# Residual folded into the gathered rows of each expert, and the pair rows summed by one constant matrix

## The chip, the cores and the metric

One Trainium2 core of one chip. The metric is the device time of the kernel in microseconds, the median of several runs.

## The reference

One decoder layer on x of 512 tokens by 1024, float32. A hybrid mixer (an input projection of 1024 by 2560, a gated linear recurrence and a short gated convolution, an output projection) is added to alpha times x and normalised, which gives h. Then the expert layer: each token picks one of four groups, two of its eight experts, and gets their weighted sum.

```
weights = softmax(top2 logits of the group) * p(group)
hid = silu(t @ w_gate[e]) * (t @ w_up[e]) * combine[:, e]
ffn = sum over the 2 chosen e of hid @ w_down[e]        # 32 experts, 1024 -> 256 -> 1024
out = layer_norm(alpha * h + ffn, ln2_g, ln2_b)         # alpha = 2 ** 0.25
```

## The kernel before, in words

The first 175 us are the mixer, in float32 split into two parts, and the router. Then TensorE builds tables of rows by products of one-hot matrices: for each expert, up to 64 tokens (`BLOCK`), each as two half rows of 512 numbers, so 128 partitions. What does not fit goes to overflow items in a loop whose count is known only at run time; it is 0 in the profiled execution.

Each of the 32 experts is an *item*, with the same instructions on every engine. `x_rows` says which rows of `h1_rows` in DRAM an item reads, `y_rows` which rows of `y_pairs` it writes. The items 0 to 9 and the last ones are written out, the others run in a hardware loop (`rounds`). On TensorE (`pe_item`, L1141) item q is: `turn_x` of item q + 1 (four transposes of the gathered rows, L1092), `gate_up` of q (L1102), `down` of q - 1 (L1131) and `turn_hid` of q (L1122). ScalarE does the silu (L841) and copies the result y to `ys` (L848). VectorE copies the transposes and multiplies hid (L1469, L1541, L1546). GpSimd gathers the rows of later items (L676, `gather`) and scatters y (L681, `scatter`), with two buffers for each; gather i + 2 waits only until x of item i has been turned. Item 0 differs: its rows come from SBUF by a product, not by a gather. In item 2 TensorE also sums the overflow tables (L1059), and VectorE takes them (`take_over`, L1523), which is the third and fourth count of `rows_ready`. VectorE computes the routing weights in item 3 (`take_weights`).

The weights of an expert are three loads of 1 MB each, issued by SP's queue: gate and up into one of eight slots (`wgu`), down into one of nine buffers (`wdn`; `wdn_once` is used by one expert only, the ninth). `refill_gu(q)` (L555) waits until gate_up of item q - 8 is done, `refill_dn(q)` (L559) until a down is done: the refills of down up to item 16 ask for one down less than the others. SP issues in the order gu8, gu9, dn9, gu10, dn10, gu11 and so on; the last ones are gu31, dn30, dn31. Behind these SP loads h1 back (2 MB), waits for a scatter of item 28 and loads the two tables of the second layer norm, then waits for all scatters and loads the 8 blocks of y_pairs (0.5 MB each). A DMA waits in the queue behind those issued before it.

The end: alpha h1 is summed into eight PSUM banks by a diagonal matrix (L1193), each pair row times its weight by eight more diagonal matrices (L1200), one of them by VectorE (L1580). Then VectorE, ScalarE and GpSimd do the layer norm tile by tile (four tiles of 128 tokens) and SP stores.

## Time and profile before

| what | value |
|---|---|
| runs | 430.11, 430.84, 432.84 us; median 430.84 |
| profiled execution | span 432.4 us; its own time is not given apart from the span |
| TensorE busy | 410.6 us (95%), mean granted clock 0.979 |
| VectorE, ScalarE, GpSimd busy | 186.8 us (43%), 114.5 (26%), 83.1 (19%) |
| DMA | 139.11 MB, 322 GB/s on average; indirect and other GpSimd DMAs 11.84 MB |
| ScalarE's copies of y (L848) | 32, 597 ns each |
| GpSimd's longest wait at the start, for the first weights | 11.1 us |
| chain that ended last | PE 82%, DMA 11%, DVE 5% |

Times are in microseconds from the start of the span. PE is the products of TensorE, PEld its weight loads, DVE VectorE, ACT ScalarE, POOL GpSimd, SP the sync engine, a q behind a name the engine's queue of DMA issues. The clock is a share of full speed (1.00 is 2.4 GHz). The DMA share of a stretch is the mean busy share of the 16 DMA engines.

### The profile page before, as it was taken

The numbers are of one execution on the slowest core, as the hardware profiler recorded it, in microseconds if no ns is written. First come the engines' busy times: TensorE is split into PE (matmuls) and PEld (weight loads), VectorE is DVE, ScalarE is ACT, GpSimd is POOL, SyncE is SP. The second block draws the span as 40 slices with busy tenths as digits, with TensorE's granted clock in tenths as the row PEclk, the third lists the DMA queues.
The fourth block names the chain that finished last, engine by engine and source line by source line (L and its number), as shares of the span: only waits on it lengthen the run. The fifth ranks groups of instructions, "written<-read, shape, count | busy, mean of one in ns | idle before, by whom it ended". The sixth has DMA issues, their size and how long they took to land.

```text
span 432.4 us, 6542 instructions
## 1 busy us (share of the span) xinstructions
PE 410.6 (95%) x2578; PEld 277.1 (64%) x2578; DVE 186.8 (43%) x368; ACT 114.5 (26%) x185; POOL 83.1 (19%) x111
## 2 busy tenths in 40 slices
PE   6999999999999999989999999999999999788883
PEld 5888877888888888955555555556555655454331
DVE  1578722499957467855322122212222221111077
ACT  3524376973122002310111111111111111003211
POOL 2201000000000001011332333233223322110124
PEclk8999999999999999998999999999999999898997
DMA  8766340230369999999999999999999999999584
GB/s 266 220 222 208 126 146 28 93 97 31 114 218 420 425 418 420 422 407 378 403 418 413 418 411 412 417 414 411 418 416 417 418 418 416 418 417 416 196 352 194
DMA packets 37377, 139.11 MB, mean 322 GB/s; under 512 B 5107, under 2 KB 17427, under 8 KB 25062
## 3 DMA queue, kind: packets, MB, share of 16 engines
q1 hardware_dynamic: 31184, 126.89, 73.7%
q0 software_dynamic: 6144, 11.84, 7.5%
q8 instruction: 18, 0.29, 0.3%
q10 hardware_dynamic: 22, 0.02, 0.0%
q14 instruction: 9, 0.07, 0.0%
HBM read 134.41 MB, written 12.58 MB: 340 GB/s over the span
## 4 chain that ended last, share of the span: by engine, by line
PE 82%; DMA 11%; DVE 5%; issue 1%; ACT 0%; SPq 0%; DVEq 0%; POOLq 0%
PE bank L1102 24%; PE bank L915 12%; PE bank L917 12%; PE bank L916 12%; PE bank L1131 11%; DMA wgu_first<-in_exp_w_up 7%; PE bank L1092 3%; PE bank L1122 3%; DMA xg<-h_rows,x_rows 2%; DVE stats L1585 1%; DMA pair_y<-y_pairs 1%; PE bank L1012 1%; DMA raw<-in_w_in 1%; PE bank L1024 1%; PE bank L975 1%; PE bank L898 1%
## 5 line engine op out<-in xcount | busy, mean ns | idle before, releaser
L1102 PE MATMUL bank<-wgu,xTg 128*64 128x256 f32 x736 | 87.7, 392 | 3.3 <-DMA wgu<-in_exp_w_up 2.4
L1102 PEld LDWEIGHTS bank<-wgu,xTg 128*64 128x64 f32 x736 | 52.6, 141 | 31.0 <-issue 3.6
L915 PE MATMUL bank<-xT_hi,w_hi 128*128 128x512 f32 x160 | 63.2, 395 | 1.8 <-DVE xT_lo L1242 1.8
L916 PE MATMUL bank<-xT_lo,w_hi 128*128 128x512 f32 x160 | 62.8, 392 | 0.0
L917 PE MATMUL bank<-xT_hi,w_lo 128*128 128x512 f32 x160 | 62.8, 392 | 0.0
L1541 DVE TENSOR_TENSOR hid<-hid,bank 64x256 f32<-64x256 f32 x32 | 13.5, 423 | 105.8 <-ACT hid L841 105.7
L681 POOL DMA_INDIRECT y_pairs<-ys,y_rows x32 | 32.5, 1016 | 134.0 <-PE bank L1092 103.6
L841 ACT ACTIVATE hid<-bank 64x256 f32<-64x256 f32 x32 | 12.1, 377 | 130.8 <-PE bank L1102 130.7
L1131 PE MATMUL bank<-wdn,hidT 128*64 128x512 f32 x192 | 45.3, 593 | 0.0
L1219 DVE TENSOR_TENSOR w_lo<-raw,w_hi 128x2048 fp32r<-128x2048 f32 x12 | 27.5, 2289 | 26.9 <-ACT w_hi L755 26.8
L676 POOL DMA_INDIRECT xg<-h_rows,x_rows x31 | 31.5, 1015 | 31.4 <-issue 19.0
L915 PEld LDWEIGHTS bank<-xT_hi,w_hi 128*128 128x128 f32 x160 | 30.2, 189 | 9.7 <-issue 3.5
L755 ACT ACTIVATE w_hi<-raw 128x2048 fp32r<-128x2048 f32 x12 | 23.0, 1916 | 45.0 <-PE bank L917 37.6
L917 PEld LDWEIGHTS bank<-xT_hi,w_lo 128*128 128x128 f32 x160 | 30.3, 190 | 6.3
L916 PEld LDWEIGHTS bank<-xT_lo,w_hi 128*128 128x128 f32 x160 | 30.2, 189 | 6.0
L848 ACT ACTIVATE ys<-bank 128x512 f32<-128x512 f32 x32 | 19.1, 597 | 46.0 <-PE bank L1131 46.0
L1546 DVE COPY hidT<-bank 128x128 f32<-128x128 f32 x32 | 9.3, 292 | 43.1 <-PE bank L1122 43.1
L1122 PEld LDWEIGHTS bank<-ident,hid 128*128 128x128 f32 x64 | 10.1, 206 | 25.6 <-DVE hid L1541 25.2
L1469 DVE COPY xTg<-bank 128x512 f32<-128x512 f32 x31 | 21.4, 692 | 7.9 <-PE bank L1092 7.9
L1131 PEld LDWEIGHTS bank<-wdn,hidT 128*64 128x64 f32 x192 | 13.7, 137 | 17.0 <-issue 13.8
L1092 PE MATMUL bank<-ident,xg 128*128 128x128 f32 x124 | 20.1, 285 | 1.8 <-DMA xg<-h_rows,x_rows 1.8
L1092 PEld LDWEIGHTS bank<-ident,xg 128*128 128x128 f32 x124 | 17.7, 211 | 1.9 <-DMA xg<-h_rows,x_rows 1.9
(253 smaller groups left out, 497.2 us busy)
## 6 DMA issues: line engine op xcount, KB each, us to landing
wgu<-in_exp_w_gate SPq DMA_DIRECT2D x24, 1024.0 KB, 19.4
wgu<-in_exp_w_up SPq DMA_DIRECT2D x24, 1024.0 KB, 22.4
wdn<-in_exp_w_down SPq DMA_DIRECT2D x24, 1024.0 KB, 22.4
raw<-in_w_in SPq DMA_DIRECT2D x9, 1024.0 KB, 5.2
raw<-in_w_out SPq DMA_DIRECT2D x4, 1024.0 KB, 5.0
wgu_spare<-in_exp_w_gate SPq DMA_DIRECT2D x4, 1024.0 KB, 22.1
wgu_spare<-in_exp_w_up SPq DMA_DIRECT2D x4, 1024.0 KB, 24.3
wdn_first<-in_exp_w_down SPq DMA_DIRECT2D x4, 1024.0 KB, 24.8
```

The costliest lines, as they stand in the source:

```text
L676: pool.indirect_dma_start(out=xg[b][:, :], out_offset=None, in_=h1_rows, in_offset=bass.IndirectOffsetOnAxis(ap=rows, axis=0), bounds_chec ...
L681: pool.indirect_dma_start(out=y_pairs, out_offset=bass.IndirectOffsetOnAxis(ap=rows, axis=0), in_=ys[b][:, :], in_offset=None, bounds_chec ...
L755: act.activation(w_hi[c][:, :], raw[c % 2][:, :], ACT.Copy).then_inc(w_hi_ready, 1)
L915: pe.matmul(dst, a_hi, b_hi, start=start, stop=False)
L916: pe.matmul(dst, a_hi, b_lo, start=False, stop=False)
L917: return pe.matmul(dst, a_lo, b_hi, start=False, stop=stop)
L1092: mm = pe.transpose(psum[b][:, j * P:(j + 1) * P], rows, ident[:, :])
L1102: mm = pe.matmul(psum[2 + b][BLOCK * which:BLOCK * which + BLOCK, 0:F], xTg[b][:, j, h * BLOCK:(h + 1) * BLOCK], wgu[s][:, which, k, :], s ...
L1122: mm = pe.transpose(psum[4 + b][:, j * P:(j + 1) * P], cols, ident[:, :])
L1131: mm = pe.matmul(psum[6 + b][BLOCK * n:BLOCK * n + BLOCK, :], hidT[b][:, j, :], wdn[s][:, j, n * H:(n + 1) * H], start=j == 0, stop=j == 1)
L1219: v.tensor_tensor(w_lo[c][:, :], raw[c % 2][:, :], w_hi[c][:, :], ALU.subtract).then_inc(w_lo_ready, 1)
L1469: v.tensor_copy(xTg[b][:, :, :], psum[b][:, :].rearrange("p (j m) -> p j m", j=4)).then_inc(xTg_ready, 1)
```

## The change

The pair rows in DRAM now hold h + (2 / alpha) w y for each of a token's two experts. Their sum is 2 / alpha times alpha h + ffn, and the layer norm takes that with its epsilon scaled by 4 / alpha squared, so h1 is not loaded back and there are no diagonals. To do so, each item keeps its gathered rows of h in place until y is added to them by VectorE (`add_y`) with a weight for each slot, and scatters the same buffer. There are eight such buffers instead of two and two `ys`; four of them lie over the routing tables (of these two in the place of the ninth down buffer), so they are cleared and gathered into only after those tables are used. The slot weights are a table that TensorE sums like the row tables, from weights cut in three bfloat16 parts. The pair rows of a token lie 64 partitions apart, and one constant matrix (`fold`) of 128 by 64 sums them. The rows of the last expert are scattered without its y, and y of the last expert is added from SBUF by products with its one-hot matrix (`last_hotT`). Loads and steps are put in another order.

```diff
-ROWS = 2
+ROWS = 8
+PARTS = 3
+HOT = 2.0 ** -7
+LAST = 31
 ...
-        wdn.append(at("wdn_once", [P, 2, D], F32, spare + 24576))
+        xg_1, xg_2 = [at(f"xg{b}", [P, H], F32, spare + 28672 + 2048 * n) for n, b in enumerate((1, 2))]
+        xg_4, xg_5 = [at(f"xg{b}", [P, H], F32, spare + 24576 + 2048 * n) for n, b in enumerate((4, 5))]
+        xg = [xg_0, xg_1, xg_2, xg_3, xg_4, xg_5, *xg_route]
 ...
             def refill_dn(q):
-                sp_.wait_ge(dn_summed, q - RING + (0 if q <= 2 * RING else 1))
-                load_dn(q, dn_slot_of(q), dn_in[dn_slot_of(q)])
-            for q in range(RING, 2 * RING + 1):
-                refill_gu(q)
-                if q > RING:
-                    refill_dn(q)
-            refill_gu(2 * RING + 1)
-            for q in range(2 * RING + 1, N_EXP):
-                if q + 1 < N_EXP:
-                    refill_gu(q + 1)
+                sp_.wait_ge(dn_summed, q - RING + 1)
+                load_dn(q, slot_of(q), dn_in[slot_of(q)])
+            refill_gu(RING)
+            refill_dn(RING)
+            refill_gu(RING + 1)
+            for q in range(RING + 1, N_EXP - 2):
+                refill_gu(q + 1)
                 refill_dn(q)
-            last_of_1 = max(q for q in range(N_EXP) if slot_of(q) == 1)
-            sp_.wait_ge(gu_summed, last_of_1 + 1)
-            sp_.dma_start(h1[:, :, :].rearrange("p t (a h) -> p t a h", a=2),
-                          h1_rows.rearrange("(t p a) h -> p t a h", p=P, a=2)).then_inc(h1_in, 16)
+            refill_dn(N_EXP - 2)
+            sp_.wait_ge(gu_summed, LAST - RING + 1)
+            for half, done in ((0, gu_in[slot_of(LAST)]), (1, last_gu_in)):
+                ks = slice(half * KT // 2, (half + 1) * KT // 2)
+                for which, w in enumerate((exp_w_gate, exp_w_up)):
+                    src = w[LAST:LAST + 1].rearrange("a (p k) f -> p (a k) f", p=P)[:, ks, :]
+                    sp_.dma_start(wgu[slot_of(LAST)][:, which, ks, :], src).then_inc(done, 16)
+            refill_dn(LAST)
 ...
-            sp_.wait_ge(y_scattered[(N_EXP - 4) % ROWS], 16 * ((N_EXP - 4) // ROWS + 1))
-            sp_.dma_start(ln2g[:, :], row(ln2_g).to_broadcast([P, D])).then_inc(ln2_in, 16)
-            sp_.dma_start(ln2b[:, :], row(ln2_b).to_broadcast([P, D])).then_inc(ln2_in, 16)
             n = sp_.value_load(n_over[0:1, 0:1], min_val=0, max_val=MAX_OVER)
             sp_.wait_ge(y_scattered[0], 16 * n + mains(0))
             for b in range(1, ROWS):
                 sp_.wait_ge(y_scattered[b], mains(b))
-            for t in range(TT):
-                for k in range(TOP_K):
-                    src = y_pairs[2 * (k * T + t * P):2 * (k * T + (t + 1) * P), :]
-                    sp_.dma_start(pair_y[t][k][:, :], src.rearrange("(p a) h -> p (a h)", a=2)).then_inc(pairs_in[t][k], 16)
+            for u in range(2 * TT):
+                if u == 4:
+                    sp_.dma_start(ln2g[:, :], row(ln2_g).to_broadcast([P, D])).then_inc(ln2_in, 16)
+                    sp_.dma_start(ln2b[:, :], row(ln2_b).to_broadcast([P, D])).then_inc(ln2_in, 16)
+                src = y_pairs[2 * u * P:2 * (u + 1) * P, :]
+                sp_.dma_start(pair_y[u][:, :], src.rearrange("(p a) h -> p (a h)", a=2)).then_inc(pairs_in[u], 16)
 ...
+            for b in (1, 2):
+                pool.memset(xg[b][:, :], 0.0).then_inc(xg_zero, 1)
 ...
-            for i in range(1, ROWS):
+            for i in range(1, 4):
                 gather(i, x_rows[:, i:i + 1])
-            SCATTER_LAG = 2
-            for i in range(N_EXP + SCATTER_LAG):
-                if i + ROWS < N_EXP:
-                    pool.wait_ge(xg_turned, i + 1)
-                    gather(i % ROWS, x_rows[:, i + ROWS:i + ROWS + 1])
-                done = i - SCATTER_LAG
-                if done == 0:
-                    pool.wait_ge(rows_ready, 2)
-                if done >= 0:
-                    pool.wait_ge(y_copied, done + 1)
-                    scatter(done % ROWS, y_rows[:, done:done + 1])
+            pool.wait_ge(rows_ready, 4)
+            for b in range(4, ROWS):
+                pool.memset(xg[b][:, :], 0.0).then_inc(xg_zero, 1)
+            for b in range(4, ROWS):
+                pool.wait_ge(xg_zero, b)
+                gather(b, x_rows[:, b:b + 1])
+            GATHER_LAG = 2
+            for i in range(N_EXP - 1):
+                if i == LAST - 3:
+                    pool.wait_ge(x_gathered[LAST % ROWS], mains(LAST % ROWS))
+                    scatter(LAST % ROWS, y_rows[:, LAST:LAST + 1])
+                pool.wait_ge(y_copied, i + 1)
+                scatter(i % ROWS, y_rows[:, i:i + 1])
+                done, new = i - GATHER_LAG, i - GATHER_LAG + ROWS
+                if done >= 0 and new < N_EXP:
+                    pool.wait_ge(y_scattered[done % ROWS], 16 * (done // ROWS + 1))
+                    gather(new % ROWS, x_rows[:, new:new + 1])
 ...
-            def copy_y(i, b, yb, scattered):
-                act.wait_ge(dn_summed, i + 1)
-                if not static(scattered) or scattered > 0:
-                    act.wait_ge(y_scattered[yb], scattered)
-                act.activation(ys[yb][:, :], psum[6 + b][:, :], ACT.Copy).then_inc(y_copied, 1)
-            def copy_main_y(q, r):
-                copy_y(q + r * RING, q % 2, q % ROWS, before(q, r))
 ...
             def act_item(q, r):
-                if static(r) and q == N_EXP - 1:
-                    make_diagonals()
-                if static(r) and q == 0:
-                    act.wait_ge(table_summed, 2)
+                if static(r) and q == LAST:
+                    act.wait_ge(last_hot_turned, 1)
+                    act.activation(last_hotT[:, :, :], psum[0][:, :].rearrange("p (t n) -> p t n", t=TT), ACT.Copy).then_inc(last_hotT_ready, 1)
                 gate(q + r * RING, q % 2, 2)
-                if q >= 1:
-                    copy_main_y(q - 1, r)
             rounds(act, act_item)
-            copy_main_y(N_EXP - 1, 0)
+            act.wait_ge(dn_summed, LAST + 1)
+            act.wait_ge(slot_weight_ready, 1)
+            act.activation(last_y[:, :], psum[6 + LAST % 2][:, :], ACT.Copy, scale=slot_weight[:, LAST:LAST + 1]).then_inc(last_y_copied, 1)
 ...
+            def sum_weights(bank, col, slots, hots):
+                for n in range(NP):
+                    for half in range(2):
+                        for c in range(PARTS):
+                            mm = pe.matmul(psum[bank][half * BLOCK:(half + 1) * BLOCK, col:col + hots.shape[3]], slots[:, n, :], hots[:, c, n, :],
+                                           start=n == 0 and c == 0, stop=n == NP - 1 and c == PARTS - 1)
+                return mm
 ...
             def pe_item(q, r):
-                if q > 1 and (not static(r) or q + 1 < N_EXP):
+                if q > 2 and (not static(r) or q + 1 < N_EXP):
                     turn_main_x(q + 1, r)
+                if static(r) and q == LAST:
+                    main_down(q - 1, r)
+                    pe.wait_ge(last_hot_ready, 1)
+                    for t in range(TT):
+                        mm = pe.transpose(psum[0][:, t * P:(t + 1) * P], last_hot[:, t, :, :].rearrange("p a n -> p (a n)"), ident[:, :])
+                    mm.then_inc(last_hot_turned, 1)
+                    gate_up(q, slot_of(q), q % 2, 2, loads_of(q, r), last_gu_in)
+                    turn_hid(q, q % 2, 2)
+                    return
                 if q == 0:
                     pe.wait_ge(gu_in[0], 32)
 ...
                     pe.wait_ge(xTg_ready, 1)
                     gate_up_first((2, 3)).then_inc(gu_summed, 1)
                     pe.wait_ge(hot_ready, 3)
-                    sum_rows(6, 0, hot_slot, hot_y).then_inc(table_summed, 1)
+                    sum_rows(7, 0, hot_slot, hot_y).then_inc(table_summed, 1)
+                    turn_hid(0, 0, 2)
                     turn_main_x(1, 0)
+                    main_down(0, 0)
                     return
                 gate_up(q + r * RING, slot_of(q), q % 2, 2, loads_of(q, r))
                 if q == 1:
-                    turn_hid(0, 0, 2)
                     turn_main_x(2, 0)
+                    turn_hid(1, 1, 2)
+                    return
                 if q == 2:
+                    turn_main_x(3, 0)
                     pe.wait_ge(over_hot_ready, 2)
                     sum_rows(3, 0, over_slot, over_x_hot)
-                    sum_rows(3, MAX_OVER, over_slot, over_y_hot).then_inc(over_summed, 1)
-                if q >= 1:
-                    main_down(q - 1, r)
+                    sum_rows(3, MAX_OVER, over_slot, over_y_hot)
+                    pe.wait_ge(hot_w_ready, 2)
+                    sum_weights(3, 2 * MAX_OVER, hot_slot_b, hot_w)
+                    sum_weights(3, 2 * MAX_OVER + N_EXP, over_slot_b, over_w).then_inc(over_summed, 1)
+                main_down(q - 1, r)
                 turn_hid(q + r * RING, q % 2, 2)
             rounds(pe, pe_item)
+            pe.wait_ge(last_hotT_ready, 1)
 ...
+            pe.wait_ge(fold_ready, 1)
+            def add_pairs(t):
+                for u in (2 * t, 2 * t + 1):
+                    pe.wait_ge(pairs_in[u], 16)
                 for h in range(2):
-                    pe.matmul(psum[2 * t + h][:, :], diag[:, 0, :], in_order(h1[:, t, :])[:, h * H // 8:(h + 1) * H // 8], start=True, stop=False)
 ...
+                    for q in range(2):
+                        pe.matmul(z_of(t, h)[BLOCK * q:BLOCK * (q + 1), :], fold[:, :], in_order(pair_y[2 * t + q][:, :], h), start=True, stop=False)
+            def add_last(t, turn):
+                if turn == 1:
+                    pe.wait_ge(last_half_added, 2 * t + 2)
+                for h in range(2):
+                    a = h ^ turn
+                    rows = slice(BLOCK * a, BLOCK * (a + 1))
+                    pe.matmul(part_of(z_of(t, h), a), last_hotT[rows, t, :], last_y[rows, h * F:(h + 1) * F],
+                              start=False, stop=turn == 1).then_inc(z_summed if turn else last_half_added, 1)
+            add_pairs(0)
+            add_pairs(1)
+            pe.wait_ge(last_y_copied, 1)
+            add_last(0, 0)
+            add_last(1, 0)
+            add_last(0, 1)
+            add_last(1, 1)
+            for t in range(2, TT):
+                add_pairs(t)
+                add_last(t, 0)
+                add_last(t, 1)
 ...
             def take_weights():
+                w = weight[:, :, :].rearrange("p k t -> p (k t)")
                 v.wait_ge(gexp_ready, 2)
 ...
                 link(v.reciprocal(weight[:, 0, :], wsum[:, :]))
-                v.tensor_tensor(weight[:, 1, :], weight[:, 0, :], vexp[:, :], ALU.mult).then_inc(weights_ready, 1)
+                link(v.tensor_scalar(weight[:, 0, :], weight[:, 0, :], 2.0 / (ALPHA * HOT), None, ALU.mult))
+                link(v.tensor_tensor(weight[:, 1, :], weight[:, 0, :], vexp[:, :], ALU.mult))
+                link(v.tensor_copy(w_parts[:, 0, :], w))
+                link(v.tensor_tensor(w_rest[:, :], w, w_parts[:, 0, :], ALU.subtract))
+                link(v.tensor_copy(w_parts[:, 1, :], w_rest[:, :]))
+                link(v.tensor_tensor(w_rest[:, :], w_rest[:, :], w_parts[:, 1, :], ALU.subtract))
+                link(v.tensor_copy(w_parts[:, 2, :], w_rest[:, :]))
+                def weighted(out, hots, n):
+                    return v.tensor_tensor(out[:, :, :, :], hots.unsqueeze(1).to_broadcast([P, PARTS, NP, n]),
+                                           w_parts[:, :, :].unsqueeze(3).to_broadcast([P, PARTS, NP, n]), ALU.mult)
+                weighted(hot_w, pairs(chosen[:, :, :, :]), N_EXP).then_inc(hot_w_ready, 1)
+                weighted(over_w, over_match[:, :, :], MAX_OVER).then_inc(hot_w_ready, 1)
+            def take_slot_weights():
+                v.wait_ge(over_summed, 1)
+                v.tensor_copy(slot_weight[:, :], psum[3][:, 2 * MAX_OVER:2 * MAX_OVER + ITEMS]).then_inc(slot_weight_ready, 1)
+                v.tensor_tensor(fold[:, :], ident[:, 0:BLOCK], ident[:, BLOCK:P], ALU.add).then_inc(fold_ready, 1)
+                v.wait_ge(slot_weight_ready, 1)
+            def find_last():
+                link(v.tensor_scalar(last_rank[:, :], last_rank[:, :], -1.0, None, ALU.add))
+                v.tensor_tensor(last_hot[:, :, :, :], up_slot.unsqueeze(1).unsqueeze(1).to_broadcast([P, TT, 2, BLOCK]),
+                                last_rank[:, :].unsqueeze(2).unsqueeze(3).to_broadcast([P, TT, 2, BLOCK]), ALU.is_equal).then_inc(last_hot_ready, 1)
 ...
+            def add_y(i, g, b):
+                v.wait_ge(dn_summed, i + 1)
+                col = slot_weight[:, i:i + 1] if static(i) else slot_weight[:, bass.ds(i, 1)]
+                v.scalar_tensor_tensor(out=xg[g][:, :], in0=psum[6 + b][:, :], scalar=col, in1=xg[g][:, :],
+                                       op0=ALU.mult, op1=ALU.add).then_inc(y_copied, 1)
+            def add_main_y(q, r):
+                add_y(q + r * RING, q % ROWS, q % 2)
             def dve_item(q, r):
                 i = q + r * RING
+                if q == 0:
+                    make_hid(0, 0, 2)
+                    copy_hidT(0, 0, 2)
+                if q == 1:
+                    find_over()
+                    take_weights()
                 if not static(r) or q + 1 < N_EXP:
                     copy_xT(i + 1, (q + 1) % 2, 2)
                 if q == 0:
                     match_over()
+                    return
                 if q == 2:
                     take_over()
-                if q == 3:
-                    take_weights()
+                    take_slot_weights()
+                    add_main_y(0, 0)
+                if static(r) and q == LAST - 2:
+                    find_last()
+                if static(r) and q == LAST:
+                    add_main_y(q - 1, r)
                 make_hid(i, q % 2, 2)
-                if q == 1:
-                    find_over()
+                if q > 1 and not (static(r) and q == LAST):
+                    add_main_y(q - 1, r)
                 copy_hidT(i, q % 2, 2)
             rounds(v, dve_item)
 ...
-                v.tensor_scalar(rstd[:, t:t + 1], moments[:, t, 1:2], LN_EPS, None, ALU.add).then_inc(var2_ready, 1)
+                v.tensor_scalar(rstd[:, t:t + 1], moments[:, t, 1:2], LN_EPS * 4.0 / ALPHA ** 2, None, ALU.add).then_inc(var2_ready, 1)
```

## Rows read from the trace of the kernel before

**Rows 1.** Page, section 2: the span in 40 slices of 10.8 us.
```profile
DMA  8766340230369999999999999999999999999584
GB/s 266 220 222 208 126 146 28 93 97 31 114 218 420 425 418 420 422 407 378 403 418 413 418 411 412 417 414 411 418 416 417 418 418 416 418 417 416 196 352 194
```

**Rows 2.** Stretches: length, busy time by engine, clock, DMA share, GB/s.
```profile
196.00:198.00 2.00, 2.00 (x10) 1.22 (x11) 1.45 (x4) 0.00 (x0) 0.77 (x1) 0.50 1.02 426
201.00:202.00 1.00, 1.00 (x10) 0.85 (x10) 0.31 (x2) 0.38 (x1) 0.00 (x0) 1.00 0.53 197
202.00:203.00 1.00, 1.00 (x6) 0.48 (x8) 0.97 (x2) 0.00 (x0) 0.29 (x1) 1.00 0.74 209
220.00:240.00 20.00, 20.00 (x154) 11.59 (x152) 4.22 (x9) 2.92 (x6) 6.77 (x7) 1.00 1.02 417
```

**Rows 3.** Chain that ended last, 195 to 222 us: start, length, what.
```profile
195.85 5.17 PE bank L1102 x32
201.02 0.43 PE bank L1122 x2
...
201.94 1.93 PE bank L1131 x8
...
208.39 0.48 PE bank L1059 x32
...
211.56 3.60 PE bank L1102 x32
...
217.80 3.60 PE bank L1102 x32
```

**Rows 4.** Timeline of SP's queue at two issues: start, length, what.
```profile
210.68 0.33 SPq L520 DMA_DIRECT2D wdn<-in_exp_w_down  x1
215.21 0.33 SPq L516 DMA_DIRECT2D wgu<-in_exp_w_gate  x1
```

**Rows 5.** Tile wgu, issues from 200.9 to 202 us (gate and up of expert 9).
```profile
DMA to landing us min/median/max: 5.9/7.1/8.3
```

**Rows 6.** Tile wgu, issues from 215 to 216 us (gate and up of expert 11).
```profile
DMA to landing us min/median/max: 9.6/10.8/12.0
```

**Rows 7.** Chain that ended last, from 365 us: start, length, what.
```profile
365.48 28.17 DMA wgu_first<-in_exp_w_up
...
398.93 1.72 PE bank L1131 x8
```

**Rows 8.** Timeline, 364 to 412 us; in brackets the idle time before and its releaser.
```profile
369.54 5.36 PE L1102 MATMUL bank<-wgu,xTg 128*64 128x256 f32 x32 [1.98 <-DMA wgu<-in_exp_w_up]
...
373.31 2.14 SPq L576 DMA_DIRECT2D h<-h_rows  x1
...
404.44 7.10 PE L1193 MATMUL bank<-h,diag 128*128 128x512 f32 x16 [0.99 <-DMA h<-h_rows]
```

**Rows 9.** Timeline, 170 to 213 us: a memset, a product, a small instruction.
```profile
170.90 0.53 POOL L667 MEMSET xg<- 128x512 f32 x1 [0.96 <-PE bank L917]
...
181.86 0.42 DVE L1450 TENSOR_TENSOR hot_x<-chosen,iota_f 128x256 f16<-128x256 f32 x1
...
212.53 0.17 DVE L1533 TENSOR_SCALAR wsum<-vexp 128x4 f32<-128x4 f32 x1
```

**Rows 10.** Tile xg, the 31 gathers.
```profile
DMA to landing us min/median/max: 6.5/7.0/8.3
```

**Rows 11.** DMA view: queue, count, median us from issue to landing.
```profile
y_pairs<-ys,y_rows POOLq DMA_INDIRECT x32, 6.6
```

**Rows 12.** Chain that ended last, 404 to 417 us: start, length, what.
```profile
404.85 3.38 DMA y_pairs<-ys,y_rows
...
413.62 1.52 DVE bank L1580 x2
415.15 1.31 DVE stats L1585 x2
```

**Rows 13.** Tile pair_y, the eight loads issued from 408.3 to 412.0 us.
```profile
DMA to landing us min/median/max: 3.9/6.9/9.2
```

More of the change, by code:

```diff
@@ L145, in hybrid_moe_layer @@
         up_block = iota_f[:, 120:120 + 1 + MAX_OVER]
+        fold = at("fold", [P, BLOCK], F32, tri_place)
+        w_parts = at("w_parts", [P, PARTS, TOP_K * TT], BF16, ones_place)
+        w_rest = at("w_rest", [P, TOP_K * TT], F32, ones_place + 64)
+        last_rank = at("last_rank", [P, TT], F32, ones_place + 96)
         first_place = place[0]
@@ L159, in hybrid_moe_layer @@
         hidT = [sb(f"hidT{b}", [P, 2, BLOCK]) for b in range(2)]
-        ys = [sb(f"ys{b}", [P, H]) for b in range(ROWS)]
-        xg = [sb(f"xg{b}", [P, H]) for b in (1, 0)][::-1]
+        xg_route = [sb(f"xg{b}", [P, H]) for b in (6, 7)]
+        xg_3, xg_0 = [sb(f"xg{b}", [P, H]) for b in (3, 0)]
         extra = sb("extra", [P, N_EXP])
@@ L292, in hybrid_moe_layer @@
         gu_in = [sem(f"gu_in{s}") for s in range(RING)]
-        dn_in = [sem(f"dn_in{s}") for s in range(RING + 1)]
+        dn_in = [sem(f"dn_in{s}") for s in range(RING)]
+        last_gu_in = sem("last_gu_in")
         over_gu_in = sem("over_gu_in")
@@ L1093, in turn_x, with gate_up @@
                 mm.then_inc(xg_turned, 1)
-            def gate_up(i, s, b, lag, loads):
+            def gate_up(i, s, b, lag, loads, late=None):
                 pe.wait_ge(gu_in[s], 32 * loads)
@@ L1100, in gate_up @@
                     h, j = divmod(k, 4)
+                    if late is not None and k == KT // 2:
+                        pe.wait_ge(late, 32)
                     for which in range(2):
@@ L1180, in pe_over @@
                 turn_hid(i, 0, 1)
-                down(i, 0, 0, 1, loads)
+                down(i, 0, 0, 2, loads)
             overflow(pe, pe_over)
             n = pe.value_load(n_over[0:1, 0:1], min_val=0, max_val=MAX_OVER)
-            pe.wait_ge(y_copied, n + N_EXP)
-            pe.wait_ge(h1_in, 16)
-            pe.wait_ge(diag_ready, 1)
-            for t in range(TT):
-                for h in range(2):
-                    pe.matmul(psum[2 * t + h][:, :], diag[:, 0, :], in_order(h1[:, t, :])[:, h * H // 8:(h + 1) * H // 8], start=True, stop=False)
@@ L1194, in _ @@
-            pe.wait_ge(diag_ready, 1 + TOP_K * TT)
-            for t in range(TT):
-                last = 0 if t < DVE_ADDED else TOP_K - 1
-                for k in range(last + 1):
-                    pe.wait_ge(pairs_in[t][k], 16)
-                    for h in range(2):
-                        mm = pe.matmul(psum[2 * t + h][:, :], diag[:, 1 + TOP_K * t + k, :], pair_y[t][k][:, h * H:(h + 1) * H],
-                                       start=False, stop=k == last)
-                        if k == last:
-                            mm.then_inc(z_summed, 1)
+            pe.wait_ge(y_copied, n + N_EXP - 1)
@@ L1575, in _ @@
             for t in range(TT):
-                if t < DVE_ADDED:
-                    v.wait_ge(pairs_in[t][1], 16)
-                    for h in range(2):
-                        v.wait_ge(z_summed, 2 * t + h + 1)
-                        step(v.scalar_tensor_tensor(out=z_of(t, h), in0=pair_y[t][1][:, h * H:(h + 1) * H], scalar=weight[:, 1, t:t + 1], in1=z_of(t, h),
-                                                    op0=ALU.mult, op1=ALU.add))
-                    v.wait_ge(dve, chain[0])
                 for h in range(2):
```

111 lines of the change are left out of this document (60 added, 51 removed).

## The prediction

> **What bounds the kernel now.** The page comes first. TensorE is busy 95% of the span, yet from the 13th to the 37th slice the DMA engines stand at 9 and move about 417 GB/s [rows 1]. Which of the two limits? While experts run, TensorE needs 6.24 us for one (starts at 211.56 and 217.80, [rows 3]); 3 MB of weights, 2.52 us per 1.05 MB at that rate, with a gather and a scatter of 0.26 MB at most need some 8.2. The chain gives most of the time to PE, but its last link before the end is a load issued at 365.48 that lands 28.17 later [rows 7], and TensorE waits 1.98 for weights before 369.54 [rows 8]. It starts late, catches up with the stream of weights and then waits for it. So the stream sets the end: a delay of TensorE costs nothing unless it empties the DMA queue, since loads are issued as slots fall free. That happens once already: at 201 to 203 the share is 0.53 and 0.74 [rows 2], 0.73 us lost, just as gu9 is issued (gu9: gate and up weights of expert 9; dn9: its down weights).
>
> How full the queue is can be read from landings. The first pair load, half of 1.05 MB on an idle queue, lands after 3.9 [rows 13], so a whole one after 5.2; the gate half of gu9 took 5.9 [rows 5]. That of gu11, issued at 215.21 [rows 4], took 9.6 [rows 6]: it had 4.4 us of work ahead of it, of which dn10, issued at 210.68 [rows 4], is 2.5.
>
> **The change, start of the experts.** The ninth down buffer, filled ahead of the experts, goes. dn8 now waits for down(0), dn9 for down(1), and dn10 for down(2), which comes behind gate_up(3) and thus behind gu11. To serve dn8, the transpose of hid(0) and down(0) move ahead of gate_up(1), where TensorE waited for gather 1 and its copy until 195.85 [rows 3]. They fit only in part, and the clock, granted 0.50 (1.2 GHz) at 196 to 198 after this idleness [rows 2], makes them slow: gate_up(1) ends near 202.8, not 201.02. Then 2.36 us (0.43 and 1.93, [rows 3]) are missing from the path to gate_up(2). VectorE does find_over (four instructions, some 1.75) and take_weights earlier: 11 small ones at 0.2 with their links (0.17 each, [rows 9]), and two products of 768 and 384 elements, at 0.42 per 256 [rows 9] less a fixed part some 1.6 together. It is free at about 203.5, so copy_xT(2), hid and the transpose follow, and gate_up(2) runs from 205.2 to 208.8, before to 208.39. last_rank adds 0.2, within this.
>
> Now item 2. Behind gate_up(2) stand turn_x(3), 0.48 (moved here from ahead of it), the over tables, 0.48 for 32 products [rows 3], and, new, 96 products of the weight tables, at the same 15 ns 1.44: done at 211.2, before at 208.87. VectorE takes two row tables, 0.45: 211.7. GpSimd waits for these (`rows_ready` 4), and behind that wait stand four memsets at 0.53 [rows 9], gathers 4 to 7 and every scatter. Gather 4 starts at 213.9. Gathers land after 6.5 to 8.3, median 7.0 [rows 10]: 220.9. TensorE needs it in turn_x(4), ahead of gate_up(3), and has only down(1) and turn_hid(2), 2.2 us, as cover: it waits some 7 us from 213.6 on. Before, gather 4 followed the turning of x 2, an item earlier, and no wait for it is listed. After the wait TensorE is slow, as at 369.54, where 32 products took 5.36 after 1.98 idle [rows 8] and not 3.60: turn 0.76, gate_up(3) 5.36, end at 227.0 against 215.17. gu11 is issued there, 11.8 later.
>
> **What that costs the stream.** The queue is empty by then: gu10 (issued 208.8) and dn9 (213.0) are through by 218.5 even with the gathers. The gate half of gu11 lands at 227.0 + 5.2 = 232.2, before at 224.8: 7.4. dn10 is behind it instead of ahead: 2.5. One gather more is already done: less 0.3. The weights are 9.6 late. From there TensorE again frees 3.15 MB each 6.24 us, more than the engines move, so the share is full, nothing is regained, and 9.6 is carried to the last weight. The smaller gaps around 200 to 210 (dn8 and gu9 late, about 3 us) are no extra: what they push back is still being moved when the large gap would begin, and shortens it.
> From below: the gather lands in 3.4, as the scatter of 404.85 did [rows 12], and the clock stays up (0.48, 3.60): gate_up(3) ends at 221.4; 1.8 + 2.5 - 0.3 = 4.0. From above: 8.3 for the gather, 5.9 for the load, the 96 products at twice the price: 3.4 more, 13.0. I take 7.0 for the gather since those of [rows 10] too were issued beside weights.
> The Trainium skill ("DMA: Bandwidth & Descriptors", Anatomy of one DMA, SWDGE path) gives a DMA 2.0 us and its bytes at 436 GB/s, an estimate of 2.6 us for such a gather. The 7.0 measured here disagrees; by the page the loss would be about 3 at full clock.
>
> **Steady items.** ACT's copies of y go; VectorE gets 31 multiply-adds of 512, 0.76 each as at L1580 [rows 12]. At 4.22 busy in 20 us [rows 2] it has room, and the add runs beside turn_hid. A scatter must land before its buffer is gathered again, which feeds an item four ahead, 25 us. TensorE has 2 us an item to spare should the strided reads of down cost something; those of L1193, strided too, cost nothing against L1200. All this: 0, and if the cover is gone, up to 2 us an item before anything shows. New memsets and iotas at the start lie in GpSimd's wait of 11.1 for the first weights. gu31 in four loads of 4 KB runs: 0, at most 0.3.
>
> **The end** (times of before; the 9.6 comes on top). dn30 goes ahead of gu31, which is split, and dn31 is last. The stream's end stays at about 399, because h1 (issued 373.31, [rows 8]) and the LN tables stood behind it. down(30) runs at 391.9, ahead of gate_up(31); its add ends at 394.45; its scatter, issued at 394.6, lands after 6.6 [rows 11]: 401.2. SP's wait for the scatters, with pair loads, tables and stores queued behind it, ends there and not at 408.29: 7.1 earlier. But the LN tables, 1 MB, now stand behind the fourth pair load, and VectorE waits for them before anything. Eight loads, issued over 4.6 us, land 3.9 to 9.2 after issue [rows 13], so one each 1.3 us: the fourth at +7.8, the tables at +10.4, that is 411.6. TensorE, idle from 401.7 to 406.3, folds: four 64-column products a tile as in down, 1.72 [rows 7], and, before tile 0 is whole, six half products for last_y (16 passes take 7.10, [rows 8], so 0.44 each), 2.6. From the fourth pair, 409.0, this is 413.3; the slow clock adds some 0.7: 414.0. Before, the statistics began at 415.15 [rows 12]; VectorE's 13.7 us from there to the last store are unchanged, and per tile the fold (3.4) just keeps up with its 3.27. The h1 products (7.10) go, but they lay under the scatter and the pair loads. Gain 1.1. At best, scatter in 3.4 and full clock: 5.0. At worst, low clock throughout: 2.0 lost.
>
> **Sum.** 9.6 - 1.1 = 8.5 on the span of 432.4 makes 440.9. The runs took 430.11, 430.84 and 432.84; the span stands 1.6 over their median, to which I carry the difference: 430.84 + 8.5 = 439.3.
>
> **Rivals.** *A small stall:* gather 4 lands in 3.4 to 4.5, the queue being short, and the clock recovers early. Loss 4.0 to 5, tail gain 1 to 3: 432 to 434.8. Against: no gather of the trace is under 6.5. Chance 0.18. The page's rule leads here too.
> *Faster:* the stream makes up for its gap, from 228 to the last weight. With gathers further ahead its rate might be the 425 GB/s of the 14th slice, not 416 [rows 1]: 3.5 us over 165. With the lowest loss (4.0) and the full tail gain (5.0) the time is 426.3. It decides if the last weights land before 399.5. Against: slices 21 to 37 lie flat at 411 to 418. Chance 0.07, a fault in my reading of the queue included.
> *No difference:* the queue never empties and only the tail counts: 429.7. For it: a dip of only 0.73 before. Against: 4.4 us of work cannot cover 11.8. Chance 0.05.
> *A larger loss:* 13.0 and a late fold: 443.8 to 446. Chance 0.10.
> The forecast, loss 7 to 12 and gain 0 to 3: chance 0.60, range 435 to 443.
>
> **Numbers.** 1% (4.3 us) is about what can be told from no change. Faster needs less than 426.5: 0.07. Slower needs over 435.15: forecast and larger loss, 0.70, and a little of the small stall, 0.72. Within 1%: 0.21. Range 432.5 to 444.0.
>
> **What would show it.** After the change: TensorE waiting 5 to 8 us for the gather of item 4 from about 214; DMA share near zero for some 7 us around 219 to 228, then 1.0 to about 408; the first pair load issued near 411; statistics from 423.6. If that wait is there and the share doesn't fall, my account of the queue is wrong; if gate_up(3) ends before 219, the chain of item 2 is.

## The result and the profile after

The changed kernel takes 440.97 us (median of 4 runs, 437.45 to 444.97) against 430.65 for the kernel before (4 runs, with those shown above): 1.0198 times as long, 95% interval 1.0143 to 1.0253. The ratio is of the fast runs and leaves out the slow one of 444.97 us, so it is below 440.97 / 430.65 = 1.0240; the median of the other three is 439.85. The profiled execution has a span of 440.2 us (its time 442.09; in the runs below, too, the time is mostly 1.7 to 2.0 above the span).

First the page after, section 2, the span in 40 slices of 11.0 us, to be held against [rows 1]:

```profile
PE   6999999999999999997399999999999999989590
DMA  8866422023279999998849999999999999999754
GB/s 263 264 191 212 163 95 91 6 95 97 95 297 424 422 420 425 395 379 335 340 159 417 413 414 412 415 416 413 415 417 417 415 418 418 415 421 372 268 217 191
```

The reader sees a hole in the plateau that was not there: the 20th and 21st slices, 209 to 231 us, at 340 and 159 GB/s, with TensorE at 7 and 3 in the 19th and 20th. After it the rate is the old one, 412 to 421. Nothing runs faster to make up for the hole.

The stretches around it, in the columns of [rows 2] (length, busy time by engine, clock, DMA share, GB/s):

```profile
202.00:206.00 4.00, 4.00 (x26) 2.40 (x27) 0.29 (x1) 0.00 (x0) 0.00 (x0) 0.66 1.01 422
206.00:210.00 4.00, 4.00 (x134) 3.05 (x132) 0.69 (x1) 0.38 (x1) 0.00 (x0) 0.91 0.45 170
210.00:216.00 6.00, 2.60 (x32) 0.95 (x26) 2.66 (x8) 0.00 (x0) 4.40 (x7) 1.00 1.01 407
216.00:218.00 2.00, 0.00 (x0) 0.00 (x0) 0.00 (x0) 0.00 (x0) 1.51 (x2) 0.74 0.89 325
218.00:220.00 2.00, 0.74 (x4) 0.73 (x4) 0.00 (x0) 0.00 (x0) 1.57 (x2) 0.50 0.49 165
220.00:222.00 2.00, 2.00 (x10) 1.01 (x10) 0.69 (x1) 0.00 (x0) 0.46 (x1) 0.50 0.27 97
222.00:224.00 2.00, 2.00 (x12) 1.10 (x10) 0.00 (x0) 0.00 (x0) 0.00 (x0) 0.55 0.00 0
224.00:226.00 2.00, 2.00 (x20) 1.17 (x18) 0.00 (x0) 0.26 (x1) 0.00 (x0) 1.00 0.00 0
226.00:228.00 2.00, 2.00 (x13) 0.90 (x10) 0.96 (x2) 0.12 (x1) 0.00 (x0) 1.00 0.54 147
```

Missing shares times lengths: 2.2 us at 206 to 210, 7.6 at 216 to 228, together 9.8, where [rows 2] had 0.73.

One more hole lies ahead of these. The same stretch in the kernel before and in the changed one:

```profile
185.00:190.00 5.00, 5.00 (x56) 3.00 (x54) 2.69 (x13) 0.00 (x0) 1.09 (x1) 1.00 1.00 415
```

```profile
185.00:190.00 5.00, 5.00 (x42) 3.01 (x40) 2.58 (x10) 0.00 (x0) 3.12 (x3) 1.00 0.78 273
```

The share of 0.78 makes 1.1 us. Here the ninth down load (issued at 175.96 before) is missing: behind dn6 SP issues nothing until the gate weights of expert 7, at 186.99, and the queue runs dry ahead of them. In all the changed kernel's stream lost 10.9, the old one 0.7: 10.2 more. The chain that ended last says why, from gate_up(2) on (start, length, what; compare [rows 3]):

```profile
202.23 5.29 PE bank L1120 x32
...
208.81 1.55 PE bank L1075 x96
...
210.54 0.24 DVE y_rows L1579
...
212.90 6.31 DMA xg<-h_rows,x_rows
...
219.26 1.13 PE bank L1108 x4
220.39 5.30 PE bank L1120 x32
225.69 1.72 PE bank L1149 x8
```

The 96 products of the weight tables (L1075), the row tables, the memsets, then gather 4 with its 6.31, and gate_up(3) at the low clock. gu11 is issued at its end:

```profile
212.14 0.33 SPq L524 DMA_DIRECT2D wdn<-in_exp_w_down  x1
225.74 0.33 SPq L538 DMA_DIRECT2D wgu<-in_exp_w_gate  x1
```

From the first of these two issues (the timeline of SP's queue; dn9 and gu11) to the second are 13.6 us, with no load between. The gate half of gu11 then lands after 4.9 us, up to 8.5 for both: an empty queue (tile wgu, that issue).

```profile
DMA to landing us min/median/max: 4.9/6.7/8.5
```

At the other end of the kernel the timeline shows the same work in another order, with TensorE and SP's queue to be held against [rows 7, 8, 12]:

```profile
394.99 3.67 PE L1120 MATMUL bank<-wgu_spare,xTg 128*64 128x256 f32 x32 [0.19 <-DMA wgu_spare<-in_exp_w_up]
...
405.10 0.98 POOL L706 DMA_INDIRECT y_pairs<-xg,y_rows  x1 [2.04 <-DVE xg L1631]
...
408.98 1.76 SPq L617 DMA_DIRECT2D pair_y<-y_pairs  x4
...
413.63 2.43 PE L1230 MATMUL bank<-pair_y,fold 128*64 128x512 f32 x8 [2.06 <-DMA pair_y<-y_pairs]
417.41 3.68 PE L1230 MATMUL bank<-pair_y,fold 128*64 128x512 f32 x8 [1.35 <-DMA pair_y<-y_pairs]
421.02 2.34 PE L1240 MATMUL bank<-last_y,last_hotT 64*128 64x256 f32 x16
423.04 1.29 DVE L1679 BATCH_NORM_STATS2 stats<-bank 128x6 f32<-128x512 f32 x2 [13.66 <-PE bank L1240]
```

gate_up(30) starts at 394.99, before at 385.85: 9.1 later in times of the span. But the experts did not start alike. These are the first products of gate_up(0), before and after:

```profile
188.01 1.04 PE L1112 MATMUL bank<-wgu,xTg 128*64 128x256 f32 x8
```

```profile
186.74 1.04 PE L1130 MATMUL bank<-wgu,xTg 128*64 128x256 f32 x8
```

The profiled execution of the changed kernel was 1.27 ahead there (in all twelve traces this start lies anywhere from 186.2 to 188.2, with no tie to the change), so from there the stream lost 10.4, which agrees with the 10.2 of the shares. The pair loads start 0.7 later than before instead of 9.1 later, but the statistics 7.9 later: the end regains 1.2 us. That is one execution against one. From gate_up(30) to the first statistics it is 29.3 before and 28.1 after, but 28.7, 27.5 and 29.6 in experiments 2, 3 and 8, which have the old end: the 1.2 is no larger than the spread.

### The profile page after: what moved, and what is told of

Read it like the earlier page. It is cut to its first block, busy times and chain, and to the rows that moved or that the text cites. A ratio compares the mean times of both kernels' runs of the same rounds, so it can differ in the third digit from the quotient of the medians.

```text
span 440.2 us, 6782 instructions
## 1 busy us (share of the span) xinstructions
PE 408.0 (93%) x2698; PEld 276.0 (63%) x2698; DVE 207.8 (47%) x410; ACT 93.8 (21%) x146; POOL 86.0 (20%) x119
## 4 chain that ended last, share of the span: by engine, by line
PE 79%; DMA 12%; DVE 5%; issue 1%; SPq 1%; ACT 0%; POOL 0%; DVEq 0%; POOLq 0%
PE bank L1120 21%; PE bank L922 12%; PE bank L923 12%; PE bank L924 12%; PE bank L1149 9%; DMA wgu_spare<-in_exp_w_up 7%; PE bank L1108 3%; PE bank L1140 3%; DMA pair_y<-y_pairs 2%; DMA xg<-h_rows,x_rows 1%; DVE stats L1679 1%; PE bank L1019 1%; DMA raw<-in_w_in 1%; PE bank L905 1%; PE bank L1085 1%
## 5 line engine op out<-in xcount | busy, mean ns | idle before, releaser
L1120 PE MATMUL bank<-wgu,xTg 128*64 128x256 f32 x736 | 89.5, 399 | 2.4 <-DMA wgu<-in_exp_w_up 2.4
L1120 PEld LDWEIGHTS bank<-wgu,xTg 128*64 128x64 f32 x736 | 53.7, 143 | 31.5 <-issue 5.1
L706 POOL DMA_INDIRECT y_pairs<-xg,y_rows x32 | 32.0, 1001 | 124.3 <-DVE xg L1631 123.3
L1269 DVE TENSOR_TENSOR w_lo<-raw,w_hi 128x2048 fp32r<-128x2048 f32 x12 | 27.5, 2289 | 26.5 <-ACT w_hi L785 26.5
L1631 DVE SCALAR_TENSOR_TENSOR xg<-bank,slot_weight,xg 128x512 f32<-128x512 f32 x31 | 23.3, 751 | 28.1 <-PE bank L1149 28.0
L1140 PE MATMUL bank<-ident,hid 128*128 128x128 f32 x64 | 16.1, 334 | 4.5 <-DVE hid L1621 4.4
```

The lines of the kernel that those rows point to most:

```text
L706: pool.indirect_dma_start(out=y_pairs, out_offset=bass.IndirectOffsetOnAxis(ap=rows, axis=0), in_=xg[b][:, :], in_offset=None, bounds_chec ...
L1120: mm = pe.matmul(psum[2 + b][BLOCK * which:BLOCK * which + BLOCK, 0:F], xTg[b][:, j, h * BLOCK:(h + 1) * BLOCK], wgu[s][:, which, k, :], s ...
L1140: mm = pe.transpose(psum[4 + b][:, j * P:(j + 1) * P], cols, ident[:, :])
L1269: v.tensor_tensor(w_lo[c][:, :], raw[c % 2][:, :], w_hi[c][:, :], ALU.subtract).then_inc(w_lo_ready, 1)
L1631: v.scalar_tensor_tensor(out=xg[g][:, :], in0=psum[6 + b][:, :], scalar=col, in1=xg[g][:, :], op0=ALU.mult, op1=ALU.add).then_inc(y_copied, 1)
```

## The experiments

All are compared with the kernel before, run beside them; ratios carry 95% intervals. The theory: what costs is the time in which the DMA queue is empty, and it is empty because gather 4 holds up gate_up(3). The main rival: the chain is right that TensorE (or the engines' added work per item) sets the time.

**1. turn_x(4) behind gate_up(3).**

```diff
-                if q > 2 and (not static(r) or q + 1 < N_EXP):
+                if q > 3 and (not static(r) or q + 1 < N_EXP):
                     turn_main_x(q + 1, r)
 ...
+                if q == 3:
+                    turn_main_x(4, 0)
```

> The changed kernel, but in item 3 TensorE does gate_up(3) first and turn_x(4) behind it, as item 2 already does with turn_x(3). Theory (the late gather empties the DMA queue): gate_up(3) no longer waits for gather 4 and ends near 216.5 instead of 225.5, gu11 is issued 9 us earlier, the stretch of no DMA traffic from 219 to 227 goes, and the time falls by 6.5 to 8, to about 433 to 435. Rival (the small stall was cheap and the loss lies in the slower steady items, VectorE's added work or the scatters): within 1 us of the changed kernel, 440 to 441.

Measured: 435.05 us (6 runs), 1.0069 [1.0036, 1.0103]. One moved step takes 1.3% (5.6 us) off the changed kernel, against 6.5 to 8 expected. The steady items are unchanged in it, so they do not hold these 5.6 us. The size is short because another wait took over, as its stretches show:

```profile
206.00:210.00 4.00, 4.00 (x138) 2.54 (x137) 2.25 (x7) 0.00 (x0) 1.15 (x3) 1.00 0.91 346
...
218.00:222.00 4.00, 4.00 (x12) 1.34 (x12) 1.11 (x2) 0.00 (x0) 0.45 (x1) 0.50 1.01 390
222.00:226.00 4.00, 4.00 (x28) 2.64 (x28) 1.64 (x3) 0.00 (x0) 1.54 (x2) 0.79 0.76 293
226.00:230.00 4.00, 4.00 (x30) 2.09 (x25) 1.12 (x3) 0.38 (x1) 0.47 (x1) 1.00 0.68 213
```

The hole shrinks from 7.6 to 2.2 us at 222 to 230. turn_x(4) still waits 3.5 us, now behind gate_up(3), and down(2) behind it runs at clock 0.50, so dn10 comes late. In all about 2.8 us of traffic is missing between 206 and 230 (and 1.0 at 185 to 190, as in the changed kernel); the run is 3.0 above the kernel before.

**2. A 7 us stall in the kernel before, where the queue is short, and 3. where it is long.** Ahead of gate_up(3), or of gate_up(9), 61 transposes that nobody needs.

```diff
+                if q == 3:
+                    keep_busy(psum[3][:, 256:384], 61)
                 gate_up(q + r * RING, slot_of(q), q % 2, 2, loads_of(q, r))
```

> The kernel before with 61 idle transposes (7.0 us) on TensorE ahead of gate_up(3), nothing else. Theory (only the emptying of the queue costs): gu11 is issued 7.0 later with 4.4 us of work in the queue, so the end moves by 2.6 (1.5 to 3.5), to about 433.3. Rival (the chain of waits is right and TensorE sets the end): 7.0 later, 437.7.

> The kernel before with the same 61 transposes ahead of gate_up(9), where loads land about 20 us after issue, so some 15 us of work is in the queue. Theory: 0 (within 0.7). Rival (TensorE sets the end): 7.0 later.

Measured: 435.12 us, 1.0073 [1.005, 1.0096], at item 3, that is 3.1 us (2.2 to 4.1) for a stall of 6.8; 431.43 us, 1.0007 [0.9983, 1.003], at item 9, so at most 1.3 us for the same stall, and nothing within the noise. The rival, 7 us in both, is out. The timeline of the two (start, length, what) shows the stalls to be equal, item 3 first, then item 9:

```profile
210.95 6.82 PE L898 MATMUL bank<-ident 128*128 128x128 f32 x61
217.70 3.67 PE L1102 MATMUL bank<-wgu,xTg 128*64 128x256 f32 x32
```

```profile
246.70 6.82 PE L898 MATMUL bank<-ident 128*128 128x128 f32 x61
253.45 3.67 PE L1102 MATMUL bank<-wgu,xTg 128*64 128x256 f32 x32
```

and the stretches tell them apart, again item 3 first:

```profile
218.00:220.00 2.00, 2.00 (x22) 1.35 (x20) 0.00 (x0) 0.00 (x0) 0.00 (x0) 1.00 0.68 277
220.00:222.00 2.00, 2.00 (x18) 1.06 (x16) 0.17 (x1) 0.38 (x1) 0.00 (x0) 1.00 0.02 8
222.00:224.00 2.00, 2.00 (x14) 1.01 (x11) 0.54 (x2) 0.60 (x1) 0.00 (x0) 1.00 0.58 209
```

```profile
245.00:255.00 10.00, 10.00 (x87) 8.53 (x85) 1.09 (x3) 0.60 (x1) 2.02 (x2) 1.00 1.02 411
255.00:265.00 10.00, 10.00 (x74) 5.31 (x70) 1.83 (x4) 1.35 (x3) 2.03 (x2) 1.00 1.01 419
```

At item 3 the engines miss 3.4 us of work, at item 9 none. The stall of 6.8 less the work in the queue (4.4, read off [rows 6]) is 2.4, at the lower end of the 3.1 (2.2 to 4.1) measured; this bears the account out, and this in the kernel before, with no part of the change.

**4. The changed kernel with its clock kept up during the wait.** 52 transposes before turn_x(4).

> The changed kernel with 52 transposes (5.9 us) on TensorE while it waits for gather 4, so that its clock stays up. Theory: gate_up(3) takes 3.7 instead of 5.4 and turn_x(4) 0.65 instead of 1.1, gu11 is issued 2.1 earlier, and the time falls by 2 (1.3 to 2.5), to about 439. Rival (the length of that stretch of TensorE does not matter, only the gather): no change, 441.

Measured: 441.51 us, 1.0229 [1.0153, 1.0304]. The interval overlaps that of the changed kernel and is too wide to exclude 2 us; taken by its time, the expectation missed. In its trace the gain is there: gate_up(3) takes 3.67 (at 220.76), and gu11 is issued 25.0 us after gu9 instead of 27.3. From the first product of gate_up(0), here at 187.71, gate_up(30) starts 2.2 earlier than in the changed kernel, and the span ends 1.5 earlier. The rest went at the end:

```profile
393.74 5.36 PE L1120 MATMUL bank<-wgu_spare,xTg 128*64 128x256 f32 x32 [1.88 <-DMA wgu_spare<-in_exp_w_up]
...
408.69 1.76 SPq L617 DMA_DIRECT2D pair_y<-y_pairs  x4
```

gate_up(30), after a wait of 1.88, runs at the low clock (5.36, not 3.67), and the pair loads, counted from the same product, are only 1.3 earlier. Whether the 1.5 us hold in most executions stays open: the four times do not show them.

**5. The start repaired.** Experiment 1, and VectorE's copies of x(2), hid(1) and its transpose before take_weights, and each gather right behind its own memset.

```diff
                 if q == 1:
                     find_over()
+                    copy_xT(2, 0, 2)
+                    make_hid(1, 1, 2)
+                    copy_hidT(1, 1, 2)
                     take_weights()
+                    return
 ...
             for b in range(4, ROWS):
                 pool.memset(xg[b][:, :], 0.0).then_inc(xg_zero, 1)
-            for b in range(4, ROWS):
                 pool.wait_ge(xg_zero, b)
```

> The changed kernel with turn_x(4) behind gate_up(3), and two more edits of the start: VectorE copies x(2) and hid(1) ahead of take_weights, and GpSimd gathers into each buffer right after its memset, not after all four. Theory (every us in which the DMA queue is empty costs one): gate_up(2) no longer waits 2.6 us for VectorE, gather 4 starts some 3 us earlier, dn10 is issued 6 us earlier, and of the 3.1 us without traffic that were left between 206 and 231 about 0.7 stay: 2.5 less than with turn_x(4) alone, within 1 us of the kernel before. Rival (what is left of the loss lies elsewhere, in VectorE's added work per item): 3 us above before, as with turn_x(4) alone.

Measured: 432.64 us (10 runs), 1.0013 [0.9991, 1.0036]. Three edits of order, all between 195 and 220 us, take the changed kernel back to within 1.6 us of the kernel before, with VectorE's adds, the weight tables, the scatters in place and the new end all left as changed. The holes from 206 on are gone (compare the stretches above):

```profile
206.00:210.00 4.00, 3.91 (x80) 2.12 (x75) 2.66 (x8) 0.00 (x0) 1.78 (x3) 1.00 0.99 369
...
222.00:226.00 4.00, 4.00 (x28) 2.12 (x26) 1.87 (x4) 0.38 (x1) 0.77 (x1) 1.00 0.99 389
226.00:230.00 4.00, 4.00 (x35) 2.30 (x32) 0.25 (x2) 0.38 (x1) 2.31 (x3) 1.00 1.00 411
```

The one that the missing ninth down load leaves is not: 1.2 us, as in the changed kernel.

```profile
185.00:190.00 5.00, 5.00 (x44) 3.20 (x44) 2.84 (x10) 0.00 (x0) 3.12 (x3) 1.00 0.76 256
```

**6. The end alone, and 7. with the start.** LN tables issued behind dn31; TensorE finishes tile 0 before it waits for the pairs of tile 1.

```diff
             refill_dn(LAST)
+            sp_.wait_ge(dn_summed, 26)
+            sp_.dma_start(ln2g[:, :], row(ln2_g).to_broadcast([P, D])).then_inc(ln2_in, 16)
+            sp_.dma_start(ln2b[:, :], row(ln2_b).to_broadcast([P, D])).then_inc(ln2_in, 16)
 ...
-            add_pairs(0)
-            add_pairs(1)
-            pe.wait_ge(last_y_copied, 1)
 ...
+            for t in range(TT):
+                add_pairs(t)
+                if t == 0:
+                    pe.wait_ge(last_y_copied, 1)
+                add_last(t, 0)
+                add_last(t, 1)
```

> The changed kernel with the end alone in another order: the two LN tables are issued behind dn31 and not behind the fourth pair load, and TensorE finishes tile 0 (fold and the last expert's y) before it waits for the pairs of tile 1. Theory (the end of the changed kernel is bound by the fourth pair load and the order of the fold): statistics start near 418 instead of 423, time 4 to 5 less, about 436.5. Rival (VectorE or the loads of the pairs set the end anyway): within 1 us of the changed kernel.

> The edits of the start and of the end together. Theory: they add up, 4 below the kernel before (3 to 5), about 427. Rival (they overlap: an earlier end of the weights lets TensorE wait and its clock fall, which takes the gain back): not over 1 us below before.

Measured: 440.56 us, 1.0194 [1.0167, 1.0221], and 432.61 us, 1.0027 [1.0002, 1.0052]. Both miss: no gain at the end. The timeline of the first:

```profile
405.26 0.99 POOL L706 DMA_INDIRECT y_pairs<-xg,y_rows  x1 [2.05 <-DVE xg L1626]
...
411.33 3.87 SPq L617 DMA_DIRECT2D pair_y<-y_pairs  x8
...
416.13 3.68 PE L1230 MATMUL bank<-pair_y,fold 128*64 128x512 f32 x8 [4.40 <-DMA pair_y<-y_pairs]
```

The last scatter is issued when it was, but the pair loads follow 6.1 us later, in the changed kernel 3.9 (405.10 to 408.98); in experiment 7, with the same end, they follow 6.0 later. The tables are still landing then (ln2b is issued at 389.41 and lands 22.1 later), so their traffic is the likely cause. Then the fold of tile 0 takes 3.68 at the low clock. What the earlier load of the tables gave was lost again at the scatter.

**8. The kernel before without its ninth down buffer.** dn8 waits for down(0) and is issued behind gu9.

> The kernel before without the ninth down buffer: dn8 waits for down(0), and each later dn for one down more. Theory: the queue, which ran dry for 0.7 us at 201 to 203, now does so 2.5 us earlier and stays dry until gu9 is issued: 2.6 later, about +0.6%. Rival (1 MB more or less ahead of the experts is absorbed, the queue being deep later): no change.

Measured: 433.06 us, 1.0027 [1.0009, 1.0045]: 1.2 us (0.4 to 1.9), less than the 2.6 expected. The sign is the theory's, the place and the size are not. In the profiled execution the stretches of 2 us from 198 to 204 have shares of 0.98 to 1.01. The hole lies earlier, where nothing is issued between dn6 (173.82) and the gate weights of expert 7 (186.49):

```profile
185.00:190.00 5.00, 5.00 (x42) 3.20 (x44) 2.92 (x11) 0.00 (x0) 2.13 (x2) 1.00 0.76 263
```

The share of 0.76 makes 1.2 us, where the kernel before has 1.00, and so has experiment 3, the same program up to item 9 (1.01). The time and the hole agree.

**9 and 10. The end in other ways, on top of 5.** Tables behind the second pair load, tile 0 first; then the same with 16 transposes before the pairs of tile 1.

> The kernel with the edits of the start, and at the end: the LN tables behind the second pair load (not the fourth), and tile 0 finished by TensorE before it waits for the pairs of tile 1. The scatters are left alone this time, since no DMA is added ahead of them. Theory: tile 0 is whole 8.8 us after the first pair load is issued (5.2 for two loads, 1.9 fold, 1.5 last y), tile 1 13.9 after it, where its statistics now start 17.0 after it: 3 less than with the edits of the start alone, about 2 below the kernel before (0.995). Rival (TensorE at the low clock sets the end, as the two tries with the tables in front showed): tile 1 is not ready before 16, gain under 1.

> The same with 16 idle transposes (1.8 us) on TensorE between tile 0 and tile 1, in the wait for the pairs of tile 1. Theory: without them the fold of tile 1 takes 3.5 at the low clock, with them 1.94: 1.5 less again, about 0.992 of the kernel before. Rival (the clock does not fall after so short a wait): no difference between the two.

Measured: 434.17 us, 1.0044 [1.0024, 1.0064], and 433.17 us, 1.0029 [1.0009, 1.005]. Neither beats experiment 5. In the first, both folds ran at the low clock:

```profile
402.10 0.82 SPq L617 DMA_DIRECT2D pair_y<-y_pairs  x2
...
406.83 3.58 PE L1231 MATMUL bank<-pair_y,fold 128*64 128x512 f32 x8 [2.12 <-DMA pair_y<-y_pairs]
...
413.66 3.58 PE L1231 MATMUL bank<-pair_y,fold 128*64 128x512 f32 x8 [1.82 <-DMA pair_y<-y_pairs]
...
418.70 1.29 DVE L1679 BATCH_NORM_STATS2 stats<-bank 128x6 f32<-128x512 f32 x2 [3.39 <-PE bank L1241]
```

The statistics of tile 1 start 16.6 after the first pair load, as with the old order (17.0), not 13.9. With the transposes the fold takes 1.94 but starts only at 415.80, 12.0 after the first pair load: then the loads of tile 1, behind the tables, are what is late; its statistics start at +15.4. The two intervals overlap. The rival of the first holds; that of the second doesn't in the trace (the clock did fall without the transposes), and the gain in time can't be told from none.

## Why the prediction was right

The measured median, 440.97, is 1.7 above the 439.3 forecast, that of the three runs in the ratio, 439.85, 0.6; by the ratio, 1.98% against 2.0%. The sign, the size and the main place were right. That the size fits this closely is in part luck: one hole of 1.1 us was not in the sum, and two errors nearly cancelled.

- *The stream sets the end, TensorE's chain does not.* Shown by experiments 2 and 3 in the kernel before: the same stall costs 3.1 us, or nothing that can be told from the noise, by the depth of the queue.
- *gather 4 holds up gate_up(3), which empties the queue.* In the trace as forecast: TensorE waits 6.57 before 219.26 (forecast 7), the share is 0 at 222 to 226, gu11 is issued at 225.74 (forecast 227.0). Shown by experiments 1 and 5: with order alone changed, first 5.6 us of the loss go and then all but 0.6 (-0.4 to +1.6).
- *The loss of the stream, 9.6.* Measured 10.2 by the shares and 10.4 by gate_up(30), counted from gate_up(0). Its make-up differed. The forecast had nothing for the 1.1 at 185 to 190: it took the ninth down load off the list and looked only at dn8 and gu9, around 200 to 210, not at what the queue still held before expert 7's weights. Experiment 8 puts 1.2 us on this. gate_up(1) ended at 198.4, not 202.8: TensorE had been idle less before it, and it ran in 3.65. But then TensorE waited 2.61 for VectorE and take_weights, so that gate_up(2) started 3.7 after the end of gate_up(1) and not 2.4, and it took 5.36 at the low clock, forecast 3.6. The forecast end of gate_up(2), 208.8, was 207.5, or 208.8 when the 1.27 by which this execution was ahead is put back: the two errors cancelled. Experiments 1 and 5 suggest that the second was worth repairing: VectorE's order is part of what separates 1.0069 from 1.0013, though none of these edits was measured alone.
- *Gather of 7.0.* It took 6.31, beside a full share (1.01 at 210 to 216), so the rows from stretches full of weights were the right neighbours. The gathers of items 5, 6 and 7, issued behind it while the queue drained, landed after 5.2, 4.2 and 3.1, and the two scatters issued at 218.12 and 219.46 after 2.5. The Trainium skill's fixed cost plus bytes ("DMA: Bandwidth & Descriptors", Anatomy of one DMA, SWDGE path), 2.6 as an estimate, agrees with these last two and not with gather 4. The small-stall rival had the effect right, but it came too late: with gather 7 and not with gather 4, for which TensorE waits.
- *The steady items cost nothing.* Experiment 5 bounds all that is left together at 0.4% above the kernel before, with the hole of 1.2 us in it and whatever the end gains. The rate is level too: 416 GB/s at a full share from 232 to 390 in the changed kernel, 417 in [rows 2].
- *The end gains 1.1.* 1.2 in the profiled execution, but of other parts: the first pair load came 8.4 us earlier than a mere shift would give (forecast 7.1), and the low clock took more from the folds. Neither trace nor times show that there is a gain: the 1.2 is within the spread of single executions. Experiment 5 is level with the kernel before although its hole of 1.2 us is left, which a gain of that size at the end would explain; no run shows it alone.
- *Wrong beyond the prediction:* in the experiments I held that the DMA time at the end was free to reorder. Experiments 6 and 7 expected 3 to 5 us there, 9 and 10 about 3 and 4.5, and none of the four showed one in its time.
- *The base.* The forecast adds its difference to the median, and so does not lean on the span of 432.4. That execution was a long one: the time of a run is some 1.8 above its span, which puts it near 434.2 as an estimate, and experiment 3, whose stall cost nothing to be seen, has a span of 429.2. The dip of 0.73 us that [rows 2] show at 201 to 203 does not occur in experiment 3 (0.98 or more in every 2 us from 184 to 240). Counted from gate_up(0), these two spans still differ by 1.6 us, and differences between two single traces are good to no more than that here.

## What to carry to other kernels

When loads are issued as buffers come free, ask of every delay how much work the DMA queue holds at that moment: landing time of a load, less that of one on an idle queue. In this kernel a delay shorter than this was free, and the rest was paid and not regained while the engines were saturated; the first few items, before the queue has filled, are where it is short. The same question goes for a load that is taken away: its work, too, covered a stretch in which nothing is issued. And a buffer that shares memory with a table moves its first gather behind the table's last reader: put the step that needs the gather as late in that item as its neighbours allow.

## What the runs showed of the hardware that was not expected

The same indirect DMA of up to 0.26 MB landed 6.3, 5.2, 4.2, 3.1 and 2.5 us after issue in the changed kernel as the queue of weights ran dry (gathers 4 to 7 and the first scatters, issued from 212.90 to 218.12): its latency follows the work that is queued at that moment. An indirect scatter at the end of the stream landed 3.3 to 3.9 us after issue (kernel before, changed kernel, experiments 1 and 5), and 6.0 to 6.1 after it when 1 MB of loads from another engine's queue had been put ahead (experiments 6 and 7).

TensorE's clock fell to its lower level (granted 0.50, 1.2 GHz) after waits as short as 1.8 to 2.1 us at the end of the kernel: a fold of eight passes then took 3.4 to 3.6 instead of 1.94 (experiments 5, 9 and 10), and in the changed kernel 3.68 after waits of 2.06 and 1.35 with 2.43 us of work between. The length of the wait alone does not decide it: the same fold kept the upper level after waits of 1.91 and 1.74 in experiment 1 and of 1.44 in experiment 5, and so did 32 products of gate_up(30) after 2.01 (experiment 1) and 1.86 (experiment 9), which took 5.36 after 1.88 in experiment 4. What does decide it stays open. With sixteen idle transposes, 1.97 us, in such a wait the fold took 1.94 (experiment 10).
